# The routed sum of a mixture of experts kept in two DRAM tensors, one for the larger and one for the smaller blocks

## What is computed

```python
def body(b, acc):                       # one block of rows of one expert
    rows = lax.dynamic_slice(row_tok, (b * EXPERT_BLOCK,), (EXPERT_BLOCK,))
    rw = lax.dynamic_slice(row_w, (b * EXPERT_BLOCK,), (EXPERT_BLOCK,))
    e = block_e[b]
    gu = x_pad[rows] @ w_gu[e]
    y = ((jax.nn.silu(gu[:, :f]) * gu[:, f:]) @ w_down[e]) * rw[:, None]
    return acc.at[rows].add(y)
...
routed = _routed_experts(xt, idx, w.astype(xt.dtype), w_gu, w_down)
shared = _swiglu(xt, sh_w_gu, sh_w_down)
return (routed + shared).reshape(B, L, D)
...
h = _layer_norm(ALPHA * h + ffn, ln_gain[i, 1], ln_bias[i, 1])
```

## Time and profile before

| what | us |
|---|---|
| median of 3 runs (1250.25 to 1254.72) | 1253.17 |
| the profiled execution | 1256.82 |
| its span (the clock of the rows) | 1255.0 |
| PE busy in the span | 1189.5 (95%) |
| DVE / ACT / POOL busy | 787.9 / 420.8 / 606.0 |
| HBM read / written | 274.38 MB / 51.00 MB |

### The profile page before, as it was taken

One profiled execution on the slowest core, in us unless ns is written; L12 is line 12 of the kernel. 1 busy time (PEld: TensorE's weight loads), 2 busy tenths in 40 slices (PEclk: granted clock), 3 DMA queues, 4 the chain that ended last, 5 costly groups with the idle time before them and its releaser, 6 DMA issues.

```text
span 1255.0 us, 22626 instructions
## 1 busy us (share of the span) xinstructions
PE 1189.5 (95%) x7122; PEld 1040.6 (83%) x7122; DVE 787.9 (63%) x1625; ACT 420.8 (34%) x582; POOL 606.0 (48%) x509
## 2 busy tenths in 40 slices
PE   6999999999999799999999999999999999999973
PEld 6897989747874399999999999999999998998931
DVE  7565657388988256666665566566566655647528
ACT  5253435353441023233333233233232232323323
POOL 5222222001657455666555666666666665756310
PEclk9999999999999999999999999999999999999997
DMA  6111111403352979999999999999999999999864
GB/s 240 51 35 51 44 41 34 184 27 135 102 169 71 278 230 352 375 364 359 370 355 366 357 351 362 358 349 367 344 352 355 343 352 338 346 350 341 282 165 175
DMA packets 83587, 317.50 MB, mean 253 GB/s; under 512 B 15989, under 2 KB 32450, under 8 KB 58594
## 3 DMA queue, kind: packets, MB, share of 16 engines
q1 hardware_dynamic: 56592, 249.50, 51.4%
q0 software_dynamic: 26656, 67.23, 21.9%
q10 hardware_dynamic: 306, 0.34, 0.1%
HBM read 274.38 MB, written 51.00 MB: 259 GB/s over the span
## 4 chain that ended last, share of the span: by engine, by line
DMA 50%; PE 24%; issue 11%; DVE 9%; ACT 3%; POOL 3%; POOLq 1%; DVEq 0%; ACTq 0%; SPq 0%
DMA routed_rows<-ysb,to_row 47%; PE bank L116 6%; PE bank L117 6%; PE bank L118 6%; PE bank L957 3%; PE bank L440 2%; POOL expert_list L787 1%; DMA win_raw<-in_w_in 1%; POOL routed_rows L840 1%; DVE routed L1440 1%; DVE h L1136 1%; DVE routed L1429 1%; DMA lists<-expert_list 1%; DVE h L1134 1%; DVE h L1120 1%
## 5 line engine op out<-in xcount | busy, mean ns | idle before, releaser
L957 PEld LDWEIGHTS bank<-xT,wgu 128*128 128x128 f32 x4096 | 516.3, 192 | 21.2 <-issue 10.4
L957 PE MATMUL bank<-xT,wgu 128*128 128x160 f32 (+1 forms) x4096 | 521.0, 288 | 10.5 <-DVE xT L1317 9.6
L810 POOL DMA_INDIRECT xg<-h_rows,from_row x288 | 324.2, 1126 | 110.6 <-issue 86.7
L840 POOL DMA_INDIRECT routed_rows<-ysb,to_row x96 | 147.8, 1540 | 215.8 <-issue 210.3
L1098 ACT ACTIVATE ysb<-bank,of_row 128x512 f32<-128x512 f32 x64 | 44.0, 687 | 439.3 <-DVE to_row L1312 381.1
L1359 DVE TENSOR_TENSOR wd_lo<-wd_raw,wd_hi 128x1024 fp32r<-128x1024 f32 x128 | 151.1, 1222 | 39.9 <-ACT wd_hi L1089 39.4
L1089 ACT ACTIVATE wd_hi<-wd_raw 128x1024 fp32r<-128x1024 f32 x128 | 127.9, 1048 | 1.4 <-issue 0.6
L787 POOL DMA_INDIRECT expert_list<-entry,place x64 | 64.7, 1010 | 129.9 <-DVE place L1197 112.2
L116 PE MATMUL bank<-hT_hi,win_hi 128*128 128x348 f32 (+1 forms) x320 | 113.4, 355 | 9.7 <-DVE hT_lo L538 9.7
L352 POOL TENSOR_TENSOR win_lo<-win_raw,win_hi 128x1024 fp32r<-128x1024 f32 x16 | 43.6, 2725 | 145.6 <-ACT win_hi L463 145.5
L1302 DVE TENSOR_TENSOR picks<-lists,pick 128x20 f32<-128x20 f32 x64 | 11.9, 185 | 161.5 <-POOLq L834 111.0
(11 more groups left out here) (216 smaller groups left out, 1629.5 us busy)
## 6 DMA issues: line engine op xcount, KB each, us to landing
wgu<-in_w_gu SPq DMA_DIRECT2D x128, 1024.0 KB
wd_raw<-in_w_down SPq DMA_DIRECT2D x64, 1024.0 KB, 8.4
win_raw<-in_w_in SPq DMA_DIRECT2D x16, 512.0 KB, 3.9
xg<-h_rows,from_row POOLq DMA_INDIRECT x288
hT_raw<-in_hT SPq DMA_DIRECT2D x8, 520.0 KB, 7.4
wout_raw<-in_w_out SPq DMA_DIRECT2D x1, 4096.0 KB, 14.4
h_in<-in_h_rows SPq DMA_DIRECT2D x8, 512.0 KB, 4.0
h_rows<-h SPq DMA_DIRECT2D x8, 512.0 KB, 2.7
```

Of the source, the lines that this page charges most:

```text
L810: pool.indirect_dma_start(out=xg[b][:, g, :], out_offset=None, in_=h1_quarters, in_offset=bass.IndirectOffsetOnAxis(ap=from_row[b][:, g:g ...
L840: pool.indirect_dma_start(out=routed_rows, out_offset=bass.IndirectOffsetOnAxis(ap=to_row[b][0:r, half:half + 1], axis=0), in_=ysb[b][0:r, ...
L957: mm = pe.matmul(bank[:, 2 * f + half, 0:BLOCK[b]], wgu[b][:, f, k, c:c + P], xT[b][:, k, 0:BLOCK[b]], start=(k == 0), stop=(k == KT - 1))
```

## The change

`routed_rows` becomes two tensors. The larger blocks (`b` = 0) add to `routed_rows[0]`, which starts as the copy of `h1` as before; the smaller ones (`b` = 1) add to `routed_rows[1]`, which POOL clears early in the mixer by a new memset of 128x512 zeros and one DMA of 4 MB that reads them 16 times. A block's addition now has to wait for the one two steps back, the last that went to the same tensor. DVE and ACT wait for that landing themselves, and `ysb_free` is gone. The tail loads both tensors, the first once the larger blocks' additions have landed, the second once the smaller ones' have. DVE adds the shared expert to six tiles first (`add_shared`, no row sum now), then the second tensor to a tile with the row sum (`add_small`, new), and fits `add_shared` of tiles 6 and 7 in ahead of the first two `finish`.

```diff
-    routed_rows = nc.dram_tensor("routed_rows", (SEQ, D), F32).ap()
+    routed_rows = [nc.dram_tensor(f"routed_rows{b}", (SEQ, D), F32).ap() for b in range(2)]
...
+    zeros = m.at("zeros", 200000, [P, D // 2], F32)
...
-    routed = m.at("routed", 0, [P, TILES, D], F32)
+    routed = [m.at(f"routed{b}", (0, 132992)[b], [P, TILES, D], F32) for b in range(2)]
...
-        pool.dma_start(sched_dram[0:HALF, :], iota_e_i[0:HALF, 0:4]).then_inc(y_stored[1], 16)
+        pool.dma_start(sched_dram[0:HALF, :], iota_e_i[0:HALF, 0:4]).then_inc(y_stored[0], 16)
+        s.step(pool.memset(zeros[:, :], 0.0))
+        pool.dma_start(routed_rows[1].rearrange("(p i) (c d) -> p (i c) d", p=P, c=2),
+                       zeros[:, :].unsqueeze(1).to_broadcast([P, 2 * TILES, D // 2])
+                       ).then_inc(y_stored[1], 16)
...
-            pool.wait_ge(y_stored[1 - b], stores_to(i, j - 1))
-            pool.sem_inc(ysb_free, 1)
+            pool.wait_ge(y_stored[b], stores_to(i, j - 2))
+            pool.sem_inc(pool_pass, 1)
...
-                    out=routed_rows,
+                    out=routed_rows[b],
...
-            act.wait_ge(ysb_free, t + 1)
+            act.wait_ge(y_stored[b], stores_to(i, j - 2))
+            act.sem_inc(act_pass, 1)
...
-            dve.wait_ge(ysb_free, t + 1)
+            dve.wait_ge(y_stored[b], stores_to(i, j - 2))
...
-        sp.wait_ge(stores_done, 1)
-        for j in range(TILES):
-            sp.dma_start(routed[:, j, :], routed_rows[cols(j), :]).then_inc(routed_ready[j], 16)
+        for b in range(2):
+            sp.wait_ge(stores_done, b + 1)
+            for j in range(TILES):
+                sp.dma_start(routed[b][:, j, :], routed_rows[b][cols(j), :]
+                             ).then_inc(routed_ready[b][j], 16)
...
         def add_shared(n):
-            b = n % 2
-            x = halves(routed[:, n, :])
+            x = halves(routed[0][:, n, :])
             c = 2 * (n % BY_BANK)
             dve.wait_ge(sh_down_done, n + 1)
-            dve.wait_ge(routed_ready[n], 16)
+            dve.wait_ge(routed_ready[0][n], 16)
             dve.scalar_tensor_tensor(x, bank[:, c:c + 2, :], 1.0 / ALPHA, x,
-                                     ALU.mult, ALU.add, accum_out=mean2[b][:, 0:1]
-                                     ).then_inc(sh_read, 1)
+                                     ALU.mult, ALU.add).then_inc(sh_read, 1)
+
+        def add_small(n):
+            b, x = n % 2, routed[0][:, n, :]
             dve.wait_ge(sh_read, n + 1)
+            dve.wait_ge(routed_ready[1][n], 16)
+            dve.scalar_tensor_tensor(x, x, 1.0, routed[1][:, n, :], ALU.mult, ALU.add,
+                                     accum_out=mean2[b][:, 0:1]).then_inc(tail_add, 1)
+            dve.wait_ge(tail_add, n + 1)
             dve.tensor_scalar(mean2[b][:, 1:2], mean2[b][:, 0:1], -1.0 / D, None, ALU.mult
                               ).then_inc(mean2_ready, 1)
...
-        add_shared(0)
+        for n in range(TILES - 2):
+            add_shared(n)
+        add_small(0)
         dve.wait_ge(lnf_loaded, 16)
         for n in range(TILES):
             if n + 1 < TILES:
-                add_shared(n + 1)
+                add_small(n + 1)
+            if n < 2:
+                add_shared(TILES - 2 + n)
             finish(n)
```

## The result

The changed kernel takes **1262.05 us** (median of 6 runs, 1259.97 to 1264.22) against 1252.32 (1249.74 to 1255.55) for the kernel before on the same chip: ratio **1.0078, 95% interval 1.0056 to 1.0100**. The forecast was 1253.1 with a range up to 1259.5. The profiled execution has a span of 1262.4 us, before 1255.0. The medians lie 9.7 us apart and the two spans only 7.4, since both profiled executions are longer than their median, that of the kernel before by 4.5 us (1256.82) and that of the kernel after by 2.2.

The account below looks back on a forecast made before the run. The prediction took the loop to be held, from near 720 us, by additions that wait for each other and fall behind PE. Loop and tail -4.2 and start +4.1 give -0.1 on 1253.17: 1253.1 us, range 1248.0 to 1259.5.

Parts of the forecast that it names:

- The loop, -9.5: Loop: with additions waiting two steps back, no wait is left and the last `down` ends 9.5 us earlier.
- carried PE's full pace to 720 with 358 GB/s: Loop: the DMA engines, full at share 1.02, kept up with PE until 720 us, and the bytes don't change.
- the additions' chain falling behind: Loop before: additions in turn take 23.7 us a pair against PE's 23.28, their head start used up near 720 us.
- Rival 3: Loop doesn't quicken: additions and gathers land later, DVE waits as before; 1262.6 us, or 1257.9 with half the waits; chance 0.08.
- What is late next is PE itself: Loop after the change: PE's `up` and `down` entries follow without a gap, larger blocks' `up` every 23.28 us.
- The start, +4.1: Start: POOL's memset and 2048-piece DMA take 6.75 us against 2.7 of cover, so PE waits 4.1 us.
- The slope of 2.7 ns a row: Start: issue cost per row from additions of 128 and 32 rows, giving 6.2 us for 2048 pieces.
- The second case: Start: the 4 MB DMA is cheap to issue and the start costs nothing; 1249.0 us in all; chance 0.26.
- The 4 MB themselves: Start: the transfer of the zeros, behind the first tile's loads with 20 us and more to spare, costs nothing.
- The tail, 59.9: Tail: from the last `down` at 1190.9 to 1250.8, DVE waiting for PE's sixth `shared_down` tile; 4.2 us kept.
- The spare of the second sum's landing: Tail: the second sum's loads have 5 us to spare, so they were costed at nothing.
- The sum: Whole kernel: -4.2 for loop and tail, +4.1 for the start, -0.1 on 1253.17, giving 1253.1 us.

Follow-up runs that it names:

- e5: Kernel after with the additions of both chains written as plain stores, so the routed sums are wrong: 1251.21 us, ratio 0.9993.
- e10: Kernel before with its additions written as plain stores, so the routed sum is wrong: 1237.63 us, ratio 0.9881.
- e4: Kernel before with gathers of 256 B a row instead of 1 KB: 1241.24 us, ratio 0.9902.
- e2: Kernel after's loop with the old tail, the second sum left out of the output: 1249.59 us, ratio 0.9968 against the kernel before.
- e6: Kernel after with shared product and second sum added tile by tile in the tail, not six shared products first: 1266.99 us, ratio 1.0110.
- e7: Kernel after with the second sum added to the first's loaded tiles by eight accumulating DMAs on POOL's queue: 1257.76 us, ratio 1.0043.
- e9: Kernel after with POOL adding the second sum in the tail, the loads of both sums alternating: 1265.16 us, ratio 1.0106.
- e1: Kernel after with one wait put back, so an addition is issued only when the one before it has landed: 1261.62 us, ratio 1.0070.
- e12: Kernel before with only the start's memset and 2048-piece DMA, into a further tensor nobody reads: 1253.24 us, ratio 1.0009.
- e11: Kernel after with the additions of the smaller blocks alone as plain stores: 1251.45 us, ratio 0.9990.
- e3: Kernel after with gathers of 256 B a row instead of 1 KB: 1249.24 us, ratio 0.9981.
- e8: Kernel after with gathers of 512 B a row instead of 1 KB: 1248.96 us, ratio 0.9976.

## Why the prediction was wrong, step by step

- **The loop, -9.5: the step that failed.** The loop was priced as if DMA engine time were free for PE's full pace once the wait between the additions was gone. That was taken from the earlier trace rows: the engines "carried PE's full pace to 720 with 358 GB/s". They did not, and the loop measured +3.2. In e5 and e10, where nothing waits, the same stretch from 460 to 720 us runs at 365 GB/s with a share of 0.98. In e5:

```profile
460.00:720.00 260.00, 260.00 (x1789) 244.13 (x1788) 165.51 (x356) 86.66 (x138) 148.45 (x135) 1.00 0.98 365
```

  At 1.02 and 358 the kernel before had 358 / 365 = 98% of that rate, and lived on work done ahead. 2% of 260 us is an estimated 5 us of lead used up. In the kernel after the lead can be seen going, in the time from issue to landing of the down weights (last number) between 460 and 560, 560 and 660, 660 and 720, 720 and 780 us:

```profile
wd_raw<-in_w_down SPq DMA_DIRECT2D x9, 1024.0 KB, 10.7
wd_raw<-in_w_down SPq DMA_DIRECT2D x8, 1024.0 KB, 13.4
wd_raw<-in_w_down SPq DMA_DIRECT2D x6, 1024.0 KB, 14.4
wd_raw<-in_w_down SPq DMA_DIRECT2D x5, 1024.0 KB, 15.6
```

  In e5 it stays at 7.6, 7.8, 7.1 and 7.6. Near 720 the lead is gone, in the kernels before and after alike. What I read as the additions' chain falling behind (12.86 + 10.85 = 23.7 us a pair) was the form in which full engines showed: an addition's 9.7 us of flight is 5.4 when it is a plain store (e10), and in e4 the chain keeps up even with 10.5 once fewer bytes are fetched. Taking the wait away handed the same lack to the weight loads, whose flight went from 8 to 16 us. Rival 3 had the sign of this, but not the mechanism: it made DVE wait as before for additions that land later. They land at a median of 10.4 for 9.7 over the whole run, and DVE doesn't wait for them. A chance of 0.08 was too little with a share of 1.02 in the row.
- **"What is late next is PE itself": wrong for the same reason.** Next was `wd_raw`. The new order is a little worse: four kernels with the same loop (e2, e6, e7, e9) have 708.6 to 709.4 us, the kernel after 711.1, and with additions in turn it is 707.7 to 707.9 (before, e1, e12). Why another 1 to 3 us are lost is not shown.
- **The start, +4.1: mis-sized.** The issue measured 1.22 us, not 6.2. The slope of 2.7 ns a row came from indirect DMAs and doesn't carry over to a direct one; the 0.74 us of the small direct DMA was the nearer row. The second case, an issue that costs nothing, stood; and by the Trainium skill, DMA: Bandwidth & Descriptors, section Anatomy of one DMA, descriptor generation is small. The trace agrees, with 1.22 us for 2048 pieces. The 4 MB themselves were costed at nothing; ACT waits 20.1 us for `win_raw` in the first 60 us where it waited 13.1, but PE does not.
- **The tail, 59.9: right**, measured 59.4 in the one trace, with PE the one waited for up to the sixth product. The spare of the second sum's landing was 2.3 us and not 5.
- **The sum.** With 59.4 for the tail, nothing for the start and 698.4 for the pairs, the span would be 1249.7; e5 and e11 are that kernel but for the adding, and have 1249.6 and 1249.5. That this agrees to 0.2 us is partly luck: their first `up` comes 1.7 us earlier and their last `down` takes 1.3 to 1.6 us longer. The forecast of the path was sound, its premise of free DMA engines was not. The start's error of 4.1 us too much hid a part of the loop's error of 12.7 too little.

## What to carry to other kernels

A DMA share of about 1.0 is a warning that the engines may be the bound, even where the compute engine shows no wait yet; here 1.02 fell behind and 1.00 did not. Compare their GB/s with what the full pace needs, ask how long the lead lasts, and see whether the time from issue to landing grows. Removing a wait then only chooses another victim, and that time shows it better than the list of waits. What helps is less engine time: fewer bytes, or a store in place of an addition, as e3, e8 and e5 showed. A second accumulator also has to be read and added at the end, and that price (about 10 us here) has to be set against what its independence buys (some 3 to 5 us in the tail, nothing in the loop).

## What the runs showed of the hardware that I had not expected

- An accumulating DMA to memory costs the DMA engines clearly more than a plain store of the same rows, by estimate 1.4 to 2.8 us of all 16 for at most 288 rows of 4 KB, while the page's counts of bytes read and written are the same for both. Its flight goes from 5.4 us to 9.7 (e10, before).
- GB/s alone does not tell whether the DMA engines are full: 358 GB/s was carried at a share of 0.97 with a loop without waits (e5, 720 to 1140 us) and at 1.02 with one that used up its lead (before, 460 to 720). The share has no sharp line either: 1.01 went with both.
- A direct DMA of 2048 pieces and 4 MB is issued by POOL in 1.22 us; one of 32 pieces took 0.74.
- DVE and POOL together on SBUF operands in the tail: 1.28 us became 2.02 in the mean for the same DVE operation.
- After the same 3.4 us without work, PE's next twelve products ran at a granted clock of 1.00 in two traces, and for the most part at 0.50 in twelve others.
